# One decoder layer: attention links moved apart in each segment, pooling products in native fp32, output products in the last segment

## What is computed

```python
xn = rmsnorm(h, g_mix); q, k, v, u = split(xn @ w_in)           # 4 x 1024 columns
q, k = rope(q), rope(k)
a = softmax(mask(q k^T * 64**-0.5))          # 16 query/key heads of 64, 8 pairs
w = a[:, :, 0] - lam * a[:, :, 1];  o = w @ v                    # 8 value heads of 128
o = rmsnorm(o, g_sub) * (1 - lam_init)
pooled = window_sum(u) / count - u           # windows 2, 4, 8, 16, a quarter of u each
pool_out = (pooled_g @ w_pool[g]) * pool_scale                   # 4 groups of 256 x 256
h = h + concat(o, pool_out) @ w_out
gate, up = split(rmsnorm(h, g_ffn) @ w_gate_up); h = h + (silu(gate) * up) @ w_down
h = h + sigmoid(rmsnorm(h, g_ple) @ w_ple_gate) * (p @ w_ple_proj)
return rmsnorm(h, g_final), k, v, last 15 rows of u
```

## Time and profile before

| | |
|---|---|
| time, median of 3 runs | 2632.21 us (2631.14 to 2632.38) |
| the profiled execution: time, span | 2630.58 us, 2628.8 us |
| TensorE matmul busy | 2492.9 us, 95% |
| TensorE weight loads busy | 2442.4 us, 93% |
| VectorE busy | 1066.8 us, 41% |
| ScalarE busy | 770.1 us, 29% |
| GpSimd busy | 128.1 us, 5% |
| mean granted TensorE clock | 0.975 of full speed |
| DMA | 271.21 MB, mean 103 GB/s |

### The profile page before, as it was taken

One profiled execution on the slowest core, in us unless ns is written; L12 is line 12 of the kernel. 1 busy time (PEld: TensorE's weight loads), 2 busy tenths in 40 slices (PEclk: granted clock), 3 DMA queues, 4 the chain that ended last, 5 costly groups with the idle time before them and its releaser, 6 DMA issues.

```text
span 2628.8 us, 46529 instructions
## 1 busy us (share of the span) xinstructions
PE 2492.9 (95%) x20153; PEld 2442.4 (93%) x20153; DVE 1066.8 (41%) x1167; ACT 770.1 (29%) x946; POOL 128.1 (5%) x72
## 2 busy tenths in 40 slices
PE   6989898897899999999999999999999999998996
PEld 5978788886899999999999999999999999998996
DVE  6354555555323433333333333334343424335332
ACT  4333334434212322222222222122212222225332
POOL 3000000000122000000000000000000000022111
PEclk9998989999999999999999999999999999999998
DMA  6443454441532233323323233332332333232232
GB/s 222 136 142 129 134 165 139 143 130 33 164 96 80 81 96 96 94 83 96 94 85 92 86 92 93 96 95 81 96 96 81 95 96 96 80 100 73 72 104 68
DMA packets 371270, 271.21 MB, mean 103 GB/s; under 512 B 5105, under 2 KB 336450, under 8 KB 370793
## 3 DMA queue, kind: packets, MB, share of 16 engines
q1 hardware_dynamic: 354243, 257.32, 32.9%
q10 hardware_dynamic: 16958, 12.91, 1.6%
HBM read 257.30 MB, written 13.37 MB: 103 GB/s over the span
## 4 chain that ended last, share of the span: by engine, by line
PE 90%; DVE 4%; ACT 4%; issue 1%; DMA 1%; SPq 0%; POOL 0%; ACTq 0%; POOLq 0%; DVEq 0%
PE acc L503 84%; PE scores L503 2%; ACT w_high L937 1%; PE mail_bank L503 1%; PE o_bank L503 1%; DVE x_low L1297 1%; DVE small L1380 1%; ACT region L1017 1%; DVE w_low L1289 0%; ACT v_now L978 0%; DMA raw<-in_w_in 0%; DVE region L1325 0%; PE mail_bank L627 0%; ACT region L1009 0%; DVE scores L1378 0%
## 5 line engine op out<-in xcount | busy, mean ns | idle before, releaser
L503 PE MATMUL acc<-x_high,w_high 128*128 128x260 f32 x4896 | 1015.9, 289 | 26.3 <-DVE x_low L1297 12.2
L503 PE MATMUL acc<-x_high,w_low 128*128 128x260 f32 x4896 | 999.8, 286 | 0.0
L503 PE MATMUL acc<-x_low,w_high 128*128 128x260 f32 x4896 | 999.7, 286 | 0.0
L503 PEld LDWEIGHTS acc<-x_high,w_high 128*128 128x128 f32 x4896 | 770.5, 193 | 43.0 <-issue 29.0
L503 PEld LDWEIGHTS acc<-x_low,w_high 128*128 128x128 f32 x4896 | 769.3, 192 | 0.0
L503 PEld LDWEIGHTS acc<-x_high,w_low 128*128 128x128 f32 x4896 | 769.3, 192 | 0.0
L1289 DVE TENSOR_TENSOR w_low<-raw,w_high 128x2048 fp32r<-128x2048 f32 x197 | 452.0, 2294 | 249.6 <-ACT w_high L937 248.6
L937 ACT ACTIVATE w_high<-raw 128x2048 fp32r<-128x2048 f32 x197 | 376.0, 1908 | 506.4 <-PE acc L503 496.8
L503 PE MATMUL acc<-act_low,w_high 128*128 128x260 f32 x1408 | 283.2, 283 | 0.0
L503 PE MATMUL acc<-act_high,w_high 128*128 128x260 f32 x1408 | 282.4, 282 | 0.0
L503 PE MATMUL acc<-act_high,w_low 128*128 128x260 f32 x1408 | 281.3, 281 | 0.0
(11 more groups left out here) (198 smaller groups left out, 1107.5 us busy)
## 6 DMA issues: line engine op xcount, KB each, us to landing
raw<-in_w_gate_up SPq DMA_DIRECT2D x88, 1024.0 KB, 5.8
raw<-in_w_down SPq DMA_DIRECT2D x44, 1024.0 KB, 5.1
raw<-in_w_in SPq DMA_DIRECT2D x32, 1024.0 KB, 6.3
key_pages<-in_cache_k SPq DMA_DIRECT2D x32, 512.0 KB, 6.2
region<-in_cache_v SPq DMA_DIRECT2D x32, 512.0 KB, 6.1
raw<-in_w_out SPq DMA_DIRECT2D x16, 1024.0 KB, 5.9
raw<-in_w_ple_gate SPq DMA_DIRECT2D x16, 1024.0 KB, 6.7
h_spill<-region ACTq DMA_DIRECT2D x1, 4160.0 KB, 13.4
```

The lines of the kernel that those rows point to most:

```text
L503: return pe.matmul(o, l, r, start=start, stop=stop)
```

## The change

- **Order of the segments.** On TensorE, ScalarE, VectorE and in `MAILS` the small steps are put in another order: k's transposes go to the front (after v's), the turned weights of block 0 before the samples' scores, and each transpose, its copy and the product that uses it get at least one fill between them. `scores` of a block follow the turned weights of the block before. On ScalarE the swap of k, the high part of u(g+1) and the high part of v(g+1) move: the swap from before the last weights' copy to behind the squares, the u slab behind the copy of the output. On VectorE the four dot products stand apart, one each after the combining of blocks 1, 2, 3 and one after the scaling of the output; the rotation of k moves behind that too.
- **SP's order.** The query rows and key pages are loaded after the value pages and the k slab; k and v slabs are no longer asked for in the same places.
- **Pooling products** leave the last segment. `mix(t)` makes tile t by four native fp32 matmuls from the unsplit `w_pool` (256 KB a group, in `w_mix`) and the unsplit pooled rows, in segments 2, 4 and 6 for tiles 0 to 5, into `acc` (the turns of `acc` are counted by `turn` and `pool_turn`); VectorE scales them back into `k_all` (`take_mixed`). Tiles 6 and 7 are made in the last segment into the scores' bank. The slab of `w_pool` and its split are gone.
- **Last segment.** After u(7) the fills are output products: `out_first` (first half of the columns, heads 0 to 6), `out_mixed` (pooled tiles 0 to 5). The second halves (`out_second`), tile 6, head 7 and tile 7 come after the segment. The samples' norm is done inside the segment by mail `norm`; the new rows' transposes are spread over the next output slabs.

The diff, cut to its core:

```diff
-         (("v", "s", "t0", "w", "pv0", "t1", "pv1", "t2", "x", "k", "t3", "o") if g < NH - 1 else
-          ("v", "s", "new", "t0", "w", "pv0", "t1", "pv1", "t2", "x", "k", "coef", "t3", "o"))]
+         (("v", "k", "t0", "s", "w", "pv0", "t1", "pv1", "t2", "x", "t3", "o") if g < NH - 1 else
+          ("v", "k", "t0", "s", "new", "w", "pv0", "t1", "pv1", "t2", "x", "t3", "coef", "norm", "o"))]
...
 SyncE, segment(g)
-                sp.wait_ge(S["multiplied"], NPG * (g + 1))
-                load_query(g + 1)
-                load_pages(g + 1, keys, k_pages, k_landed, (S["dotted"], NPG * (g + 1)))
                 load_u(g + 1)
+                load_pages(g + 1, pages_v, v_pages, v_landed, (S["mail_ready"], MAIL["x", g] + 1))
                 if g < NH - 2:
                     load_k(g + 2)
-                load_pages(g + 1, pages_v, v_pages, v_landed, (S["mail_ready"], MAIL["x", g] + 1))
-                if g < NH - 2:
+                    sp.wait_ge(S["multiplied"], NPG * (g + 2))
+                    load_query(g + 2)
+                    load_pages(g + 2, keys, k_pages, k_landed, (S["dotted"], NPG * (g + 2)))
                     load_v(g + 2)
+                if g in (2, 4):
+                    sp.wait_ge(S["acc_ready"], pool_turn(g - 1) + 1)
+                    load_mix(g // 2)
...
 TensorE, new
+            def mix(t):
+                g, m = divmod(t, 2)
+                if m == 0:
+                    pe.wait_ge(S["mix_landed"], 16 * (g + 1))
+                    pe.wait_ge(S["u_taken"], 4 * g + 4)
+                if t < MIXED:
+                    pe.wait_ge(S["acc_free"], pool_turn(t) - 1)
+                    pair = acc[pool_turn(t) % 2]
+                else:
+                    pe.wait_ge(S["exped"], 4 * NH)
+                    pair = sc
+                    if m:
+                        pe.wait_ge(S["pooled_low"], t)
+                for a in (0, 1):
+                    for k in (0, 1):
+                        at = k * 2 * P + m * P
+                        ins = mm(pair[:, a, 0:HT], w_mix[g // 3][:, at:at + P],
+                                 k_all[:, 2 * g + k, a * HT:(a + 1) * HT], start=k == 0, stop=k == 1)
+                ins.then_inc(S["acc_ready"] if t < MIXED else S["mixed_ready"], 1)
```

More of the change, by code:

```diff
@@ L576, in dense @@
                 if n == 0:
-                    begin(slab, i, i < 2)
-                part_of(slab, acc[i % 2], i, (2 * n, 2 * n + 1), x_waits(0) if i == 0 else None)
+                    begin(slab, turn(i), i < 2)
+                ins = part_of(slab, acc[turn(i) % 2], turn(i), (2 * n, 2 * n + 1), x_waits(0) if i == 0 else None)
+                if i == u_slab(NH - 1) and n == KD // 4 - 1:
+                    ins.then_inc(S["x_read"], 1)
             for n in range(KD // 2):
@@ L694, in turn_o, with spread_norms @@
                 ins.then_inc(S["mail_ready"], 1)
+            def mix(t):
[17 more added lines that the diff above has]
+                ins.then_inc(S["acc_ready"] if t < MIXED else S["mixed_ready"], 1)
+            def spread_norms():
+                pe.wait_ge(S["onew_squared"], 1)
+                mail_turn("norm", NH - 1)
+                mm(mbank[:, 0:64], ones, v_squares[:, 0:64]).then_inc(S["mail_ready"], 1)
             def segment(g, fill):
                 scores(g, 0)
-                fill(0)
+                if g in (2, 4, 6):
+                    mix(g - 2)
+                else:
+                    fill(0)
                 v_natural(g)
-                fill(1)
+                if g in (2, 4, 6):
+                    mix(g - 1)
+                else:
+                    fill(1)
+                k_natural(g)
+                if g in (2, 4, 6):
+                    fill(0)
+                else:
+                    fill(2)
+                turn_w(g, 0)
+                if g in (2, 4, 6):
+                    fill(1)
+                    fill(2)
+                fill(3)
                 turn_sample_scores(g)
-                fill(2)
+                scores(g, 1)
+                fill(4)
+                values(g, 0)
                 if g == NH - 1:
                     new_scores()
[L706 to L709, removed]
                 fill(5)
@@ L771, in out_part, with out_first @@
-            def out_part(m, ks):
-                slab = Slab(OUT_N + m)
[L774 to L778, removed]
+            def out_first(m, k):
+                slab = Slab(OUT_N + m)
+                w_high, w_low = (w[slab.slot][:, k * P:(k + 1) * P] for w in (wh, wl))
+                pe.wait_ge(S["o_low_done"], k + 1)
+                mm(acc[m][:, 0, 0:HT], w_high, xh[:, k, 0:HT], start=k == 0, stop=False)
+                mm(acc[m][:, 0, 0:HT], w_high, xl[:, k, 0:HT], start=False, stop=False)
+                mm(acc[m][:, 0, 0:HT], w_low, xh[:, k, 0:HT], start=False, stop=False)
@@ new lines, in out_second, with out_both @@
+            def out_second(m, k):
+                slab = Slab(OUT_N + m)
+                w_high, w_low = (w[slab.slot][:, k * P:(k + 1) * P] for w in (wh, wl))
+                mm(acc[m][:, 1, 0:HT], w_high, xh[:, k, HT:T], start=False, stop=False)
+                mm(acc[m][:, 1, 0:HT], w_high, xl[:, k, HT:T], start=False, stop=False)
+                mm(acc[m][:, 1, 0:HT], w_low, xh[:, k, HT:T], start=False, stop=False)
+            def out_both(m, k):
+                slab = Slab(OUT_N + m)
+                w_high, w_low = (w[slab.slot][:, k * P:(k + 1) * P] for w in (wh, wl))
+                for n, (w, x) in enumerate(((w_high, xh), (w_high, xl), (w_low, xh))):
+                    for a in (0, 1):
+                        ins = mm(acc[m][:, a, 0:HT], w, x[:, k, a * HT:(a + 1) * HT],
+                                 start=a == 1 and k == NH and n == 0, stop=k == KD - 1 and n == 2)
+                return ins
@@ L780, in last_fill, with out_mixed @@
+            def out_mixed(m, *ts):
+                for t in ts:
+                    pe.wait_ge(S["pooled_low"], t + 1)
+                    out_both(m, NH + t)
             def last_fill(i):
@@ L1065, in segment @@
                 store_v(g)
+                k_natural(g)
+                take("t0", g, w_turn[0][:, 0:P], mbank[:, 0:P])
+                fill(0)
                 sample_exp(g)
                 exps(g, 1)
-                fill(0)
-                take("t0", g, w_turn[0][:, 0:P], mbank[:, 0:P])
                 if g == 0:
@@ L1077, in segment @@
                 take("t1", g, w_turn[1][:, 0:2 * P], mbank[:, 0:2 * P])
+                exps(g, 2)
+                fill(2)
                 take("pv1", g, pv[:, 512:1024], mbank[:, :])
-                fill(2)
-                exps(g, 3)
                 fill(3)
@@ L1635, in norm_low @@
                 V.wait()
-            for j in (0, 1):
+            for j in (0, 1, 2):
                 out_step(j, 0)
```

340 lines of the change are left out of this document (193 added, 147 removed).

## The result

The changed kernel takes 2543.38 us (median of 4 runs, 2542.54 to 2544.51) against 2632.3 before: the ratio is 0.9654, with a 95% interval of 0.963 to 0.9679. The forecast was 2555 with a range of 2538 to 2590, so the direction and the mechanism held and the gain, 88.9 us, was 12 larger than forecast. The profiled execution has a span of 2540.7 us, 88.1 less than before.

What follows compares the result with a forecast made beforehand. Bound: TensorE plus answers it asks for too soon, with the clock adding. Savings 9.9 + 45.4 + 27.5 - 1.9 = 80.9, less 4 for small waits: 77 off 2630.6, median 1.6 above: 2555 us, range 2538 to 2590.

Steps and rivals of the forecast that it cites:

- The bound: Attention segments: TensorE's own 48.15 us each plus answers it asks for too soon; the clock falls after such waits.
- The walk: Timed list of one segment's steps on each engine; TensorE ends at 48.3 us if nothing waits, all three waits go.
- the longest link: Segment end: ScalarE's output copy, then high and low part of the next slab, ready 0.95 us before TensorE asks.
- The mixing's wait: Segments 2, 4, 6: first dense fill waits 0.65 us for VectorE to take the first pooling tile.
- The clock: Segments: 0.85 us each kept for lower clock at the near-empty own-values products, bounds 0 and 3.5; last stretch 1.7.
- The allowance: Whole kernel: 4 us taken off the summed saving for waits under 1 us that step-by-step timing misses.
- The first segment: The 7.59 us wait behind VectorE's eight dot operations stays; the segment takes 49.7 for 59.6, saving 9.9 us.
- The last stretch: From segment 7's scores: 68.1 us against 95.6, saving 27.5, with waits of 0.9, 1.7, 4.0 and 3 to 5.
- The long link: Rival, chance 0.15: end-of-segment chain or the root's chain overruns, TensorE waits 3 us in seven segments, 2588 us.
- The clock that doesn't come back: Rival, chance 0.09: transposes and near-empty products lower the clock without waits, segments keep 0.94 to 0.89, 2576 us.
- Waits that only move: Rival, chance 0.04: each gap reappears elsewhere, segments gain nothing and the six tiles cost 12.5 us, 2619 us.
- Late key pages: Slower rival, chance 0.04: key pages asked for after the fourth dot product land late, TensorE waits; 2640 us if 30 late.

Runs made afterwards that it cites:

- the second experiment: Changed kernel with ScalarE doing the exps of block 3 before copying the turned weights of block 2, in every segment: 2578.04 us.
- invert_first: Changed kernel with one pair swapped on VectorE, the sums inverted ahead of adding the samples' new terms in the last segment: 2538.76 us.
- slab_early: Changed kernel with one load moved: SP asks for the third output slab right behind the second, not after the last pooled tile: 2538.06 us.
- before_copy_first: Kernel before with one link moved: in segments 0 to 6 ScalarE copies the last turned weights before k's swap and the next u slab's high part: 2613.33 us.

## Why the prediction was right, and where it was off

*The bound.* It said that a segment is PE's own 48.15 us plus the links asked for too soon. An undisturbed pair of neighbouring segments takes 100.23 us; less two pooling tiles (3.5) and one wait of 0.51 that is 48.1 each. This is shown, and shown again by the links put back one at a time: the waits come back at their places, each with its price.

*The walk.* All 21 waits were forecast to go, and they went. The margin at the longest link was 1.26 for 0.95. The mixing's wait was 0.51 for 0.65; the pair's extra is 3.9 us for 4.15. Segments 2, 4 and 6 were to take 52 to 54 us from v to v and took 51.9, since the first of the two tiles falls into the stretch before.

*The clock.* This is the largest term that was mis-sized. I kept 0.85 us per segment for falls behind the own values, 6 in all. There were none: the granted clock of segments 1 to 6 is 1.00 with the near-empty products in place, and in segment 0 (0.96) only the first 4 us, behind the 7.4, run at the lower level. The same 2 us of products with a wait of 2.1 ahead of them do bring the fall (the second experiment). I had also priced a fall at 1.7 us; behind the restored waits it was 2.4 and 2.7.

*A slip in the sum.* 48.15 and 0.85 are 49.00; the 49.15 took the 48.3 of the walk. That put 0.9 us too much into six segments.

*The allowance.* The 4 us for small waits that a walk misses were not there.

*The first segment.* The 7.59 stayed as 7.4, as forecast. Segment 0 came out 1.1 shorter than forecast, and the stretch up to its v transposes 1.6 shorter, which nothing in the change explains: before that point both kernels run the same order on PE. The start of that row ranged from 173.2 to 174.7 us over the traces of the changed order, and was 174.0 in the one of the old order with one link moved, so it isn't the change. Of the 1.6, 0.5 is there when PE gets past its wait for the page table (10.77 us before, 10.27 after). The other 1.0 comes from the first dense products: their pairs start 0.43 us apart, and not 0.24, until 50.9 us before and until 48.3 after. This part of the gain was luck for the forecast.

*The last stretch.* The forecast saved 27.5 and 25.1 came. The waits stand where the walk had them, at 0.28, 1.53, 3.72 and 5.99 us, for 0.9, 1.7, 4.0 and 3 to 5. Two terms were too small. One is the clock, put at 1.7 for the stretch: behind the waits of 1.53 and 3.72 it cost about 3.6, an estimate from the pairs behind 553.86, which start 0.43 apart in place of 0.24, and from the rows behind 572.27, set against the same rows in `invert_first`. The other is the last wait: the slab was asked for at 580.0 and split from 589.09, 9 us for a landing that I had taken as 6 from the median of such loads, though p and the end of the reload of h were on the same queues. `slab_early` shows this part by itself: the wait fell from 5.99 to 2.73.

*The sum.* 11.2 us of span beyond the forecast are 4.0 (allowance), 6.0 (clock), 1.6 (start), 1.1 (the rest of segment 0), 0.9 (the slip) and 0.7 (mixing), less 2.4 (last stretch) and 0.7 (behind it), to 0.1 us of rounding.

*The rivals.* The long link: its margin was positive in every segment. The clock that doesn't come back: refuted by 1.00. Waits that only move: refuted by the trace and by `before_copy_first`. Late key pages: no row of PE waits for them, with 175 GB/s in segment 1 for 145.

*What stays open.* How much of the last stretch's 25 us belongs to the output products' new places and how much to the small steps' new order was not taken apart. Nor was the price of the pooling tiles against tiles of split products in the same places tried; a tile took 1.76 us in the trace (272.99 to the k transposes at 274.75 in segment 2), as forecast, and the 1.44 of split products stands on the earlier trace rows alone.

## What to carry to other kernels

Where one engine is the bound and others answer it through in-order queues, write one period of the schedule as a list of times, one column for each engine, and look for every place where the bound engine asks before the answer is there. Put work between question and answer, not faster answers. Then count the wait twice: here a wait of 2.1 us on TensorE, ahead of 2 us of near-empty products, cost another 2.7 us of lower clock, one of 5.1 between dense products another 2.4, so that two exchanged lines were worth 35 us of 2578.

## What the runs showed of the hardware that I had not expected

Eight near-empty products (2 columns each, 1.84 to 2.0 us) left the granted clock at 1.00 in segments 1 to 6 of the changed kernel. Waits of 2.1 ahead of them (`exps_before_copy2`) brought it down to 0.94 to 0.97 of a segment. The three waits of 0.51 did nothing. In the kernel before, the wait of 1.8 at the last weighted values was followed by pairs 0.43 us apart in segments 0, 2, 3 and 6, which took 59.3 to 61.6 us, and by pairs 0.24 apart in segments 1, 4 and 5, which took 57.8. With the waits gone, DMA moved 162 to 201 GB/s in segments 0 to 5 and 130 in segment 6, in place of 139 to 145 in the segments of the earlier trace rows, with no wait of PE behind it, but single loads of 1 MB took longer: the median landing of the w_in slabs went from 6.3 to 9.0 us.
